# Opening three weight units of the next stage before the barrier of each norm of h, in a four-stage fp32 model kernel on one core

## Chip, cores and metric

One Trainium2 chip, one core. The metric is the device time of one execution in microseconds, lower is better. 0.3% of this kernel's time is about 5.8 us.

## The reference, cut to what matters

The input is one sequence of 512 tokens of width 1024. Four blocks run one after the other on the residual h, and each begins with an RMS norm of h:

```
h = x
h = h + ssd_mixer(rmsnorm(h) ...)                 # stage "ssd"
h = h + gla_mixer(rmsnorm(h) ...)                 # stage "gla"
h = rmsnorm(h, final_norm)                        # the end of the first block
u = rms_norm(h, norm_mix_g)                       # the second block: stages "mixp", "att", "merge"
h = h + (gates0 * conv(u) + gates1 * mla(u)) @ w_out
h = h + cross_attention(rms_norm(h), rms_norm(mem))   # stage "cross"
h = h + relu(rms_norm(h) @ w1)**2 @ w2                # stage "mlp"
out = rms_norm(h)
```

At the end of the gla stage two norms follow each other: `final_norm` (it changes h itself) and the norm of the second block.

## The kernel before

**Tiling.** h is held as 8 row tiles of 128 channels by 512 tokens. Every product with a weight matrix runs in units: one unit is up to 128x1024 weights (8 slices k of 128x128, or 4 slices for 256 output channels). A value is split into a rounded high part and the rest, so one product is three matmuls per slice (`mm3`, lines 63 to 67; low by high, high by low, high by high). A unit with 8 slices is thus 24 matmuls of 512 columns.

**The weight stream.** Units have one global order. SyncE (SP) loads unit n into one of RAW = 2 raw buffers (`load_unit`, L105), once the unit two before it has been split. ScalarE (ACT) rounds it into one of WS = 3 high buffers (`split_hi`, L115), once it has landed and the unit three before it has been multiplied. VectorE (DVE) forms the rest (`split_lo`, L126). TensorE (PE) multiplies it (`stream_products`, L145) into one of SB = 3 PSUM banks in turn, once the tile three before it has been read out. A call for a unit that is already loaded, split or streamed does nothing.

**Stages.** Each stage is one block in which every engine has its own program in a hand-written order. Between stages stand a clearing of semaphores and a barrier of all engines (`stage_semaphores`, L47 to 57), so an engine goes on only when all have come. A stage's loads and splits may reach past its end, into units of the next stage.

**A norm of h between stages.** While the last tiles of h come in, ACT makes u_hi = h * gain (`scale_tile`, L229) and squares h (`square_tile`, L191), DVE makes u_lo (`scale_rest`, L235), and GpSimd (POOL) adds the squares (`add_squares`, L203, L206). The gain is applied before the product; the reciprocal root of the mean square (rstd) is applied when a product is read out of PSUM. `next_products` (L239 to 245) then runs on PE:

- unit nx.n of the next stage, slice by slice as u_lo comes;
- a product of the sum of squares with ones (two passes of an fp32 matmul, L244), which waits for POOL;
- unit nx.n + 1.

Beside that, `next_rough` (L248) has ACT take the root (Ln, Exp) and split unit nx.n + 3, and `next_fine` (L259) has DVE refine it in four steps (`refine_rstd`, L167 to 177) and split unit nx.n + 3. Then comes the barrier. So there are four such places, called A to D here: A from ssd to gla, B from gla to mixp, C from merge to cross, D from cross to mlp.

**gla, where A ends.** Slot (0,0) of PE holds unit nx.n + 1 (query), slot (0,1) unit nx.n + 2 (key), slots (0,2) and (0,3) the first two value units. In slot (0,0) PE also runs the products for the log gates (L1332), with a small weight that SP loads at the stage's start, behind a memset on POOL (L1264 to 1266, L1271). From them ACT and DVE make decays, gated queries and keys, and their high and low parts (L1418 to 1433, L1554 to 1590). DVE reads the first value tile out behind that (L1511), and only then does PE, in slot (0,3), turn that tile (L1343) and run the attention products.

**gla, where B begins.** Place B has its own code. Two sums of squares are kept (c.sumsq and qs), DVE joins them in ks (L1639), PE multiplies both with ones (L1377, L1378), ACT takes two roots (L1475 to 1481), and DVE refines both, one after the other, before the barrier.

**mixp, where B ends.** POOL multiplies the 8 tiles of h by the first norm (L1762), beside DVE. Slot k of DVE reads tile k - 1 out (L1833), splits unit n0 + k + 2 and then does a step of the rotary angles (L1839 to L1861) or, in slots 5 and 7, of the latent norms. ACT squares tile k - 1 (L1794) ahead of its split of unit n0 + k + 2. PE's slot 4 ends with the sums of the latent squares (L1777), and slot 7 with a product with the rotated key (L1783), which needs the sine table and DVE's L1878 to 1884.

Of the kernel before, what the change touches and what calls it, by code (L numbers as in the profile page):

```python
# [21 lines left out]
D = 1024  # L22
KT = D // P
# [142 lines left out]

def refine_rstd(dve, done, n, r, tmp, sums, width, eps=EPS):  # L167
# [71 lines left out]
def next_products(c, pe, nx):  # L239

    stream_products(c, pe, nx.n, lambda j: c.uh[:, j, :], lambda j: c.ul[:, j, :],
                    ready=lambda j: (c.v_rest, nx.v + j + 1))
    pe.wait_ge(c.square_added, nx.squares)
    pe.matmul(c.q[0][:, :], c.ones[:, :], c.sumsq[:, :], start=True, stop=True).then_inc(c.summed, 1)  # L244
    stream_products(c, pe, nx.n + 1, lambda j: c.uh[:, j, :], lambda j: c.ul[:, j, :])
# [159 lines left out]
def ssd_stage(nc, c, A, plan, gain):  # L405
# [8 lines left out]
    with ExitStack() as ctx:  # L414
# [304 lines left out]
        with nc.Block() as block:  # L719
            @block.sync  # L720
            def _(sp):
                for n in range(first, c.next_unit + 4):
                    load_unit(c, sp, n)
# [479 lines left out]
def gla_stage(nc, c, A, plan, gain, gains):  # L1203
# [10 lines left out]
    with ExitStack() as ctx:  # L1214
# [45 lines left out]
        with nc.Block() as block:  # L1260
            @block.sync
            def _(sp):
# [3 lines left out]
                for n in range(first, c.next_unit + 4):  # L1266
# [13 lines left out]
            def _(pe):  # L1280
# [22 lines left out]
                for i, k in slots:  # L1303
# [21 lines left out]
                    if k == 0:  # L1325
# [43 lines left out]
                    if 8 <= k <= 13:  # L1369
                        if k < 13:  # L1370
# [3 lines left out]
                stream_products(c, pe, nx.n, lambda j: c.uh[:, j, :], lambda j: c.ul[:, j, :],  # L1374
                                ready=lambda j: (c.v_rest, nx.v + j + 1))
                pe.wait_ge(s_both, 1)
                pe.matmul(q[0][:, :], c.ones[:, :], c.sumsq[:, :], start=True, stop=True)  # L1377
                pe.matmul(q[1][:, :], c.ones[:, :], ks[:, :], start=True, stop=True).then_inc(c.summed, 1)  # L1378
                stream_products(c, pe, nx.n + 1, lambda j: c.uh[:, j, :], lambda j: c.ul[:, j, :])

            @block.scalar
            def _(act):
# [3 lines left out]
                for i, k in slots:  # L1386
# [4 lines left out]
                    if pi == GH and pk >= 10:  # L1391

                        for j in range(2):
                            final = free_value(c, tile_of(pi, pk) + j)
                            scale_tile(c, act, nx, (pk - 10) * 2 + j, final)
                            square_tile(c, act, (pk - 10) * 2 + j, final)
# [75 lines left out]
                for n in (nx.n + 1, nx.n + 2):  # L1472
# [3 lines left out]
                act.activation(c.sumsq[:, :], q[0][:, :], ACT.Ln, scale=1.0 / D, bias=c.eps[:, 0:1])\  # L1476
                   .then_inc(s_first, 1)
                act.wait_ge(c.rooted, 2 * nx.ones + 1)
                act.activation(c.rstd, c.rstd, ACT.Exp, scale=-0.5).then_inc(c.rooted, 1)
                act.wait_ge(s_first, 1)  # L1480
                act.activation(c.sumsq[:, :], c.sumsq[:, :], ACT.Exp, scale=-0.5).then_inc(s_first, 1)
# [3 lines left out]
            def _(dve):  # L1485
# [151 lines left out]

                dve.wait_ge(c.square_added, nx.squares)
                dve.scalar_tensor_tensor(out=ks[:, :], in0=c.sumsq[:, :], scalar=EPS, in1=qs[:, :], op0=ALU.mult,  # L1639
                                         op1=ALU.add).then_inc(s_both, 1)  # L1640
                for n in (nx.n + 1, nx.n + 2):
                    split_lo(c, dve, n)
                dve.wait_ge(c.rooted, 2 * nx.ones + 2)
                refine_rstd(dve, c.refined, nx.fine, c.rstd, c.newton, q[1][:, :], D, EPS * EPS)
                dve.wait_ge(s_first, 2)
                refine_rstd(dve, c.refined, nx.fine + 4, c.sumsq[:, :], c.newton, q[0][:, :], D)
# [1349 lines left out]
```

## Time and profile before

| | |
|---|---|
| three runs | 1918.66, 1920.49, 1925.13 us; median 1920.49 us |
| the profiled execution | 1918.41 us, span 1916.7 us |
| busy share of the span | PE 92%, weight loads of PE 74%, DVE 62%, ACT 40%, POOL 21% |
| mean granted clock of PE | 0.962 of 2.4 GHz |
| HBM | 135.7 MB read, 72 GB/s over the span |

The profile is one execution, in microseconds from the span's start. In a row of the timeline stand the start, the duration, the engine, the line, the operation, its tiles, how many are merged, and in brackets how long the engine had been idle and what ended that. Matmuls overlap: the duration of one is longer than the distance to the next. "PEq L57" as a releaser is the barrier.

### The profile page before, as it was taken

The numbers are of one execution on the slowest core, as the hardware profiler recorded it, in microseconds if no ns is written. First come the engines' busy times: TensorE is split into PE (matmuls) and PEld (weight loads), VectorE is DVE, ScalarE is ACT, GpSimd is POOL, SyncE is SP. The second block draws the span as 40 slices with busy tenths as digits, with TensorE's granted clock in tenths as the row PEclk, the third lists the DMA queues.
The fourth block names the chain that finished last, engine by engine and source line by source line (L and its number), as shares of the span: only waits on it lengthen the run. The fifth ranks groups of instructions, "written<-read, shape, count | busy, mean of one in ns | idle before, by whom it ended". The sixth has DMA issues, their size and how long they took to land. (4 is left out here: it accounts for less than half of the span.)

```text
span 1916.7 us, 21367 instructions
## 1 busy us (share of the span) xinstructions
PE 1764.0 (92%) x8104; PEld 1424.9 (74%) x8104; DVE 1187.6 (62%) x1580; ACT 773.6 (40%) x1140; POOL 405.8 (21%) x351
## 2 busy tenths in 40 slices
PE   5989999999977989999997799999899999999997
PEld 4767787777755767878785577888678778888886
DVE  6768877887866646474744675777565553434343
ACT  5433443344324344444433344445444442323232
POOL 0444743564363000000000601222031020000001
PEclk9989999999988898999997899999999999999999
DMA  3312222222201312222221232222323223333331
GB/s 98 89 43 58 65 66 66 64 63 73 56 24 33 85 50 66 77 66 77 67 77 37 60 88 58 67 69 58 99 88 99 88 79 99 98 91 97 99 99 67
DMA packets 252188, 139.18 MB, mean 73 GB/s; under 512 B 25965, under 2 KB 246550, under 8 KB 252086
## 3 DMA queue, kind: packets, MB, share of 16 engines
q1 hardware_dynamic: 252086, 137.82, 25.3%
q8 instruction: 65, 1.06, 0.2%
q14 instruction: 37, 0.30, 0.1%
HBM read 135.70 MB, written 2.10 MB: 72 GB/s over the span
## 5 line engine op out<-in xcount | busy, mean ns | idle before, releaser
L65 PE MATMUL stream<-u_lo,weights_hi 128*128 128x512 f32 (+2 forms) x1312 | 528.7, 403 | 20.5 <-DVE h L1028 5.0
L67 PE MATMUL stream<-u_hi,weights_hi 128*128 128x512 f32 (+2 forms) x1312 | 516.6, 394 | 0.0
L66 PE MATMUL stream<-u_hi,weights_lo 128*128 128x512 f32 (+2 forms) x1312 | 516.5, 394 | 0.0
L133 DVE TENSOR_TENSOR weights_lo<-weights_raw,weights_hi 128x1024 fp32r<-128x1024 f32 (+4 forms) x266 | 335.7, 1263 | 287.1 <-ACT weights_hi L123 287.0
L123 ACT ACTIVATE weights_hi<-weights_raw 128x1024 fp32r<-128x1024 f32 (+4 forms) x266 | 268.4, 1010 | 487.8 <-PE stream L67 455.3
L65 PEld LDWEIGHTS stream<-u_lo,weights_hi 128*128 128x128 f32 (+2 forms) x1312 | 249.7, 190 | 87.3 <-issue 18.9
L66 PEld LDWEIGHTS stream<-u_hi,weights_lo 128*128 128x128 f32 (+2 forms) x1312 | 249.3, 190 | 53.9 <-issue 2.7
L67 PEld LDWEIGHTS stream<-u_hi,weights_hi 128*128 128x128 f32 (+2 forms) x1312 | 248.4, 189 | 55.0 <-issue 0.2
L203 POOL COPY h_sum_of_squares<-h_squares 128x512 f32<-128x512 f32 x5 | 3.2, 649 | 829.0 <-ACT h_squares L191 829.0
L65 PE MATMUL stream<-mlp_a_lo,weights_hi 128*128 128x512 f32 x256 | 100.2, 391 | 0.0
L67 PE MATMUL stream<-mlp_a_hi,weights_hi 128*128 128x512 f32 x256 | 99.7, 389 | 0.0
L66 PE MATMUL stream<-mlp_a_hi,weights_lo 128*128 128x512 f32 x256 | 99.6, 389 | 0.0
L736 POOL TENSOR_TENSOR ssd_y<-ssd_y,ssd_state_parts 128x384 f32<-128x384 f32 x32 | 33.0, 1033 | 184.0 <-DVE ssd_state_parts L1045 181.7
L1962 POOL TENSOR_TENSOR mix_conv<-mix_conv,att_tap_products 128x512 f32<-128x512 f32 x30 | 40.2, 1342 | 125.2 <-ACT att_tap_products L2072 123.2
L1059 DVE SCALAR_TENSOR_TENSOR ssd_bc<-stream,params,ssd_bc 128x510 f32<-128x510 f32 (+1 forms) x64 | 48.0, 749 | 28.6 <-ACT ssd_bc L934 26.9
L2841 DVE SCALAR_TENSOR_TENSOR mlp_relu<-stream,h_squares 128x512 f32<-128x512 f32 x32 | 22.1, 691 | 70.0 <-PE stream L67 69.1
L206 POOL TENSOR_TENSOR h_sum_of_squares<-h_sum_of_squares,h_squares 128x512 f32<-128x512 f32 x34 | 48.5, 1427 | 75.4 <-ACT h_squares L191 73.8
L65 PE MATMUL stream<-ssd_y_lo,weights_hi 128*128 128x512 f32 x128 | 53.3, 416 | 8.0 <-DVE ssd_y_lo L1167 5.2
L816 PE MATMUL q<-ssd_m,ssd_x_pair 128*128 128x128 f32 x256 | 37.2, 290 | 22.9 <-DVE ssd_m L1142 22.9
L2137 DVE SCALAR_TENSOR_TENSOR q<-mix_z,params,q 128x512 f32<-128x512 f32 x76 | 57.1, 751 | 1.7
L816 PEld LDWEIGHTS q<-ssd_m,ssd_x_pair 128*128 128x128 f32 x256 | 33.4, 198 | 31.1 <-DVE ssd_m L1142 30.2
L65 PE MATMUL stream<-gla_y_lo,weights_hi 128*128 128x512 f32 x128 | 50.9, 398 | 5.8 <-DVE gla_y_lo L1594 5.8
(472 smaller groups left out, 3185.2 us busy)
## 6 DMA issues: line engine op xcount, KB each, us to landing
weights_raw<-in_w_mlp_dram SPq DMA_DIRECT2D x64, 512.0 KB, 4.0
weights_raw<-in_ssd_w_in_dram SPq DMA_DIRECT2D x48, 512.0 KB, 3.9
weights_raw<-in_gla_w_in_dram SPq DMA_DIRECT2D x40, 512.0 KB, 3.7
weights_raw<-in_w_in_dram SPq DMA_DIRECT2D x29, 512.0 KB, 3.7
weights_raw<-in_ssd_w_out_dram SPq DMA_DIRECT2D x16, 512.0 KB, 3.7
weights_raw<-in_gla_w_out_dram SPq DMA_DIRECT2D x16, 512.0 KB, 3.3
weights_raw<-in_w_out_dram SPq DMA_DIRECT2D x8, 512.0 KB, 3.8
weights_raw<-in_w_xkv_dram SPq DMA_DIRECT2D x8, 512.0 KB, 4.0
```

Source lines behind the costliest of these rows:

```text
L65: pe.matmul(out, lh, rl, start=first, stop=False, skip_group_check=skip)
L66: pe.matmul(out, ll, rh, start=False, stop=False, skip_group_check=skip)
L67: return pe.matmul(out, lh, rh, start=False, stop=last, skip_group_check=skip)
L123: act.activation(w_view(c, n)[0], raw_view(c, n), ACT.Copy).then_inc(c.w_rounded, 1)
L133: dve.tensor_tensor(lo, raw_view(c, n), hi.bitcast(F32), ALU.subtract).then_inc(c.w_split, 1)
L206: pool.tensor_tensor(acc[:, :], acc[:, :], c.sq[:, n % 2, :], ALU.add).then_inc(c.square_added, 1)
L736: pool.tensor_tensor(y[:, p, a], y[:, p, a], parts[:, d * (T - P):(d + 1) * (T - P)], ALU.add).then_inc(s_fin, 1)
L816: last = pe.matmul(q[p][:, t * P:(t + 1) * P], xp[:, t, p, a], mm[:, t % 2, 2 * p + h, :], start=h == 0, stop=h == 1, skip_group_check=True)
L1059: ins = dve.scalar_tensor_tensor(out=dst[:, a:b], in0=src[:, a + o:b + o], scalar=tap(tp, ct), in1=dst[:, a:b], op0=ALU.mult, op1=ALU.add)
L1962: pool.tensor_tensor(acc[:, LAST, :], acc[:, LAST, :], prod[:, e % 2, :], ALU.add)\
L2137: dve.scalar_tensor_tensor(out=dst, in0=src, scalar=par[:, w:w + 1], in1=q[4][:, :], op0=ALU.mult, op1=ALU.add).then_inc(s_tap, 1)
L2841: dve.scalar_tensor_tensor(out=r_[:, m % 2, :], in0=bank(c, t)[:, :], scalar=0.0, in1=c.rstd, op0=ALU.max, op1=ALU.mult).then_inc(c.bank_f ...
```

## The change

At places A, C and D PE now opens two units at once: slices 0 to 6 of unit nx.n, slices 0 to 5 of unit nx.n + 1, the product with ones, and then the slices left over. After that it streams a third unit, nx.n + 2, before the barrier (at C this is a key unit of the memory, 256 columns wide). At B the two units are opened likewise, then half of the third, the two products with ones (the joined one first), and the other half. ACT's split of unit nx.n + 2 moves ahead of the last two squares there, DVE's splits of nx.n + 1 and nx.n + 2 ahead of the join, and the refinement of the first norm moves behind the barrier, into slot 2 of mixp; the steps of the angles in slots 2 and 3 move to slots 3 and 4. POOL's multiplications of h and PE's first latent sum wait for that refinement. SP loads one unit more ahead in each of the stages. In the first round of gla the products for the log gates stand in slot 1 instead of slot 0.

```diff
+def stream_steps(c, pe, n, xh, xl, ks, ready=None):
+    kt, cols, _, _, rows = c.units[n]
+    t = c.tiles_before[n]
+    hi, lo = w_view(c, n)
+    if ks[0] == 0:
+        pe.wait_ge(c.w_split, n + 1)
+        if t >= SB:
+            pe.wait_ge(c.bank_free[t % SB], t // SB)
+    for k in ks:
+        if ready:
+            pe.wait_ge(*ready(k))
+        last = mm3(pe, bank(c, t)[0:rows, :], hi[:, k, 0:rows], lo[:, k, 0:rows], xh(k), xl(k), k == 0, k == kt - 1)
+    if ks[-1] == kt - 1:
+        last.then_inc(c.tile_done, 1)
+        c.streamed = n + 1
...
-def next_products(c, pe, nx):
-    stream_products(c, pe, nx.n, lambda j: c.uh[:, j, :], lambda j: c.ul[:, j, :],
-                    ready=lambda j: (c.v_rest, nx.v + j + 1))
+def next_products(c, pe, nx, third=None):
+    uh, ul = (lambda j: c.uh[:, j, :]), (lambda j: c.ul[:, j, :])
+    ready = lambda j: (c.v_rest, nx.v + j + 1)
+    stream_steps(c, pe, nx.n, uh, ul, range(KT - 1), ready)
+    stream_steps(c, pe, nx.n + 1, uh, ul, range(KT - 2), ready)
     pe.wait_ge(c.square_added, nx.squares)
     pe.matmul(c.q[0][:, :], c.ones[:, :], c.sumsq[:, :], start=True, stop=True).then_inc(c.summed, 1)
-    stream_products(c, pe, nx.n + 1, lambda j: c.uh[:, j, :], lambda j: c.ul[:, j, :])
+    stream_steps(c, pe, nx.n, uh, ul, range(KT - 1, KT), ready)
+    stream_steps(c, pe, nx.n + 1, uh, ul, range(KT - 2, KT), ready)
+    if third:
+        third()
+    else:
+        stream_products(c, pe, nx.n + 2, uh, ul)
...
-                for n in range(first, c.next_unit + 4):
+                for n in range(first, c.next_unit + 5):
                     load_unit(c, sp, n)
...
-                    if k == 0:
+                    if k == (0 if g else 1):
                         if g:
                             pe.wait_ge(s_on, 4 * g)
...
+                stream_steps(c, pe, nx.n, uh, ul, range(KT - 1), ready)
+                stream_steps(c, pe, nx.n + 1, uh, ul, range(KT - 2), ready)
+                stream_steps(c, pe, nx.n, uh, ul, range(KT - 1, KT), ready)
+                stream_steps(c, pe, nx.n + 1, uh, ul, range(KT - 2, KT), ready)
+                stream_steps(c, pe, nx.n + 2, uh, ul, range(KT // 2))
                 pe.wait_ge(s_both, 1)
-                pe.matmul(q[0][:, :], c.ones[:, :], c.sumsq[:, :], start=True, stop=True)
                 pe.matmul(q[1][:, :], c.ones[:, :], ks[:, :], start=True, stop=True).then_inc(c.summed, 1)
-                stream_products(c, pe, nx.n + 1, lambda j: c.uh[:, j, :], lambda j: c.ul[:, j, :])
+                pe.matmul(q[0][:, :], c.ones[:, :], c.sumsq[:, :], start=True, stop=True).then_inc(s_first, 1)
+                stream_steps(c, pe, nx.n + 2, uh, ul, range(KT // 2, KT))
...
                             scale_tile(c, act, nx, (pk - 10) * 2 + j, final)
+                            if pk == 13 and j:
+                                split_hi(c, act, nx.n + 2)
...
+                for n in (nx.n + 1, nx.n + 2):
+                    split_lo(c, dve, n)
                 dve.wait_ge(c.square_added, nx.squares)
                 dve.scalar_tensor_tensor(out=ks[:, :], in0=c.sumsq[:, :], scalar=EPS, in1=qs[:, :], op0=ALU.mult,
                                          op1=ALU.add).then_inc(s_both, 1)
-                for n in (nx.n + 1, nx.n + 2):
-                    split_lo(c, dve, n)
                 dve.wait_ge(c.rooted, 2 * nx.ones + 2)
                 refine_rstd(dve, c.refined, nx.fine, c.rstd, c.newton, q[1][:, :], D, EPS * EPS)
-                dve.wait_ge(s_first, 2)
-                refine_rstd(dve, c.refined, nx.fine + 4, c.sumsq[:, :], c.newton, q[0][:, :], D)
+                c.first_fine = nx.fine + 4
                 split_lo(c, dve, nx.n + 3)
...
+                pool.wait_ge(c.refined, c.first_fine + 4)
                 for m in range(KT):
                     pool.tensor_tensor(c.h[:, m, :], c.h[:, m, :], c.sumsq[:, :], ALU.mult).then_inc(s_first, 1)
...
                         pe.wait_ge(s_sq, (3, 5)[e])
+                        if e == 0:
+                            pe.wait_ge(c.refined, c.first_fine + 4)
...
                     if k == 2:
+                        refine_rstd(dve, c.refined, c.first_fine, c.sumsq[:, :], c.newton, q[0][:, :], D)
+                    if k == 3:
                         dve.wait_ge(s_tb, 3)
...
-                    if k == 3:
+                    if k == 4:
                         dve.wait_ge(s_tb, 7)
...
-                next_products(c, pe, nx)
+                def memory_product():
+                    pe.wait_ge(s_mlo, KT)
+                    stream_products(c, pe, nx.n + 2, lambda j: memh[:, j, :], lambda j: meml[:, j, :], MEM)
+
+                next_products(c, pe, nx, memory_product)
```

## Rows read from the trace of the kernel before

**Rows 1.** The page's first part: busy time and share of each engine.

```profile
PE 1764.0 (92%) x8104; PEld 1424.9 (74%) x8104; DVE 1187.6 (62%) x1580; ACT 773.6 (40%) x1140; POOL 405.8 (21%) x351
```

**Rows 2.** PE's waits: line, releaser, us in total, times, longest.

```profile
PE stream L65 <- PEq L57: 9.7, 4, 3.8
...
PE stream L65 <- DVE u_lo L235: 4.5, 4, 2.5
...
PE q L244 <- POOL h_sum_of_squares L206: 0.4, 2, 0.3
```

**Rows 3.** Timeline of PE at place A.

```profile
621.56 0.39 PE L67 MATMUL stream<-u_hi,weights_hi 128*128 128x512 f32 x1
627.17 3.75 PE L1332 MATMUL q<-gla_gl,gla_w_gates 32*128 32x512 f32 x4 [5.22 <-DMA gla_w_gates<-in_gla_w_gate_dram]
630.85 0.80 PE L65 MATMUL stream<-u_lo,weights_hi 128*128 128x512 f32 x1
...
646.56 0.39 PE L65 MATMUL stream<-u_lo,weights_hi 128*128 128x512 f32 x1
...
647.24 0.39 PE L65 MATMUL stream<-u_lo,weights_hi 128*128 128x512 f32 x1
...
650.49 0.65 PE L1343 MATMUL q<-ident,gla_v 128*128 128x128 f32 x4 [0.37 <-DVE gla_v L1511]
...
654.43 0.48 PE L65 MATMUL stream<-u_lo,weights_hi 128*128 128x512 f32 x1
```

**Rows 4.** Timelines of DVE and POOL at place A.

```profile
614.06 2.30 DVE L133 TENSOR_TENSOR weights_lo<-weights_raw,weights_hi 128x1024 fp32r<-128x1024 f32 x1
...
623.10 0.94 POOL L1271 MEMSET gla_w_gates<- 32x1024 f32 x1 [7.82 <-POOLq L57]
```

**Rows 5.** Stretches: from:to, us, busy us per engine (times), PE's granted clock, DMA.

```profile
628.00:637.00 9.00, 9.00 (x19) 5.50 (x18) 5.04 (x6) 4.84 (x7) 0.00 (x0) 0.53 0.56 152
...
1089.00:1094.00 5.00, 5.00 (x13) 3.89 (x14) 1.76 (x3) 1.52 (x2) 4.77 (x6) 0.51 0.79 189
```

**Rows 6.** Timeline of PE at place B and at the rotated key.

```profile
1074.99 2.07 PE L1377 MATMUL q<-h_sum_of_squares,ones 128*128 128x512 f32 x2 [3.03 <-DVE gla_k L1639]
...
1088.79 0.76 PE L65 MATMUL stream<-u_lo,weights_hi 128*128 128x512 f32 x1 [3.82 <-PEq L57]
...
1130.31 1.13 PE L1783 MATMUL q<-mixp_key_rope,mixp_join 128*128 128x512 f32 x2 [1.85 <-DVE mixp_key_rope L1884]
```

**Rows 7.** Timelines of DVE and POOL at place B and in mixp.

```profile
1080.62 0.69 DVE L170 TENSOR_SCALAR h_squares<-q 128x512 f32<-128x512 f32 x1 [4.55 <-ACT h_squares L1479]
...
1086.43 1.22 DVE L133 TENSOR_TENSOR weights_lo<-weights_raw,weights_hi 128x1024 fp32r<-128x1024 f32 x1
1088.64 0.69 DVE L1833 TENSOR_TENSOR mixp_latent<-stream,h_squares 128x512 f32<-128x512 f32 x1 [0.99 <-PEq L57]
1092.54 1.32 DVE L1839 CAST mixp_angle<-mixp_positions 128x512 f32<-128x512 int32 x1 [3.20 <-DMA mixp_rope_rows<-in_rope_rows_dram]
1093.89 1.40 DVE L1841 TENSOR_SCALAR mixp_angle<-mixp_angle,mixp_rope_rows 128x512 f32<-128x512 f32 x1
...
1107.24 0.48 DVE L1854 TENSOR_SCALAR mixp_angle<-mixp_angle,mixp_rope_rows 128x512 f32<-128x512 f32 x1
...
1129.56 0.69 DVE L1884 TENSOR_TENSOR mixp_key_rope<-mixp_key_rope,h_squares 128x512 f32<-128x512 f32 x1
...
1089.82 11.55 POOL L1762 TENSOR_TENSOR h<-h,h_sum_of_squares 128x512 f32<-128x512 f32 x8
```

**Rows 8.** Timeline of PE at places C and D.

```profile
1459.89 1.02 PE L244 MATMUL q<-h_sum_of_squares,ones 128*128 128x512 f32 x2
...
1467.48 0.36 PE L65 MATMUL stream<-mix_mem_lo,weights_hi 128*128 128x256 f32 x1 [1.08 <-PEq L57]
...
1470.42 0.28 PE L65 MATMUL stream<-mix_mem_lo,weights_hi 128*128 128x256 f32 x1
...
1562.76 0.47 PE L65 MATMUL stream<-u_lo,weights_hi 128*128 128x512 f32 x1 [1.02 <-PEq L57]
```

More of the change, by code:

```diff
@@ L1265, in _ @@
                     sp.dma_start(wg[16 * d:16 * d + 16, d, :], A["gla_w_gate"][0][d]).then_inc(s_gl["w"], 16)
-                for n in range(first, c.next_unit + 4):
+                for n in range(first, c.next_unit + 5):
                     load_unit(c, sp, n)
@@ L1372, in _ @@
                         inter(g, k - 8)
-                stream_products(c, pe, nx.n, lambda j: c.uh[:, j, :], lambda j: c.ul[:, j, :],
-                                ready=lambda j: (c.v_rest, nx.v + j + 1))
+                uh, ul = (lambda j: c.uh[:, j, :]), (lambda j: c.ul[:, j, :])
+                ready = lambda j: (c.v_rest, nx.v + j + 1)
+                stream_steps(c, pe, nx.n, uh, ul, range(KT - 1), ready)
[3 more added lines that the diff above has]
+                stream_steps(c, pe, nx.n + 2, uh, ul, range(KT // 2))
                 pe.wait_ge(s_both, 1)
-                pe.matmul(q[0][:, :], c.ones[:, :], c.sumsq[:, :], start=True, stop=True)
                 pe.matmul(q[1][:, :], c.ones[:, :], ks[:, :], start=True, stop=True).then_inc(c.summed, 1)
-                stream_products(c, pe, nx.n + 1, lambda j: c.uh[:, j, :], lambda j: c.ul[:, j, :])
+                pe.matmul(q[0][:, :], c.ones[:, :], c.sumsq[:, :], start=True, stop=True).then_inc(s_first, 1)
+                stream_steps(c, pe, nx.n + 2, uh, ul, range(KT // 2, KT))
             @block.scalar
@@ L1475, in _ @@
                 act.activation(c.rstd, q[1][:, :], ACT.Ln, scale=1.0 / D, bias=c.eps[:, 1:2]).then_inc(c.rooted, 1)
-                act.activation(c.sumsq[:, :], q[0][:, :], ACT.Ln, scale=1.0 / D, bias=c.eps[:, 0:1])\
-                   .then_inc(s_first, 1)
                 act.wait_ge(c.rooted, 2 * nx.ones + 1)
@@ L1480, in _ @@
                 act.wait_ge(s_first, 1)
+                act.activation(c.sumsq[:, :], q[0][:, :], ACT.Ln, scale=1.0 / D, bias=c.eps[:, 0:1])\
+                   .then_inc(s_first, 1)
+                act.wait_ge(s_first, 2)
                 act.activation(c.sumsq[:, :], c.sumsq[:, :], ACT.Exp, scale=-0.5).then_inc(s_first, 1)
@@ L2235, in _ @@
                 sp.dma_start(rows[:, :, :], A["mem_2"][0].rearrange("(t p) d -> p t d", p=P)).then_inc(s_min, 16)
-                for n in range(n0, n0 + N + 4):
+                for n in range(n0, n0 + N + 5):
                     load_unit(c, sp, n)
@@ L2446, in _ @@
             def _(sp):
-                for n in range(n0, n0 + N + 4):
+                for n in range(n0, n0 + N + 5):
                     load_unit(c, sp, n)
```

## The prediction, made before the changed kernel ran

> **What bounds the kernel now.** I read the page's first part [rows 1]: PE is busy for 92% of the span, so a time that falls has to come out of PE's idle 8% or its clock. PE's waits come next [rows 2]: the four barriers that end in a streamed unit cost 9.7 us, the late rests of u at places B and D 4.5 us, POOL's squares 0.4 us. These are what the change can win. Then I read the timelines around the four places, to see what PE meets after each barrier, and the question there is always the same: does PE set the pace behind the barrier, or does a chain on DVE and ACT that starts at the barrier? Only in the first case is a unit that was streamed early worth its time.
>
> The unit of the sums: one slice (three matmuls of 512 columns) takes 647.24 - 646.56 = 0.68 us [rows 3], so a unit of 8 takes 5.44 us. No work is removed or added by the change, apart from waits; everything below is order.
>
> **Place A, ssd to gla.** Before, PE ends at 621.56 + 0.39 = 621.95 and the next stage starts at 623.10 [rows 3, 4]. Then PE waits until 627.17 for the gate weights, 4.07 us behind the barrier: their DMA is issued inside the stage, behind POOL's memset. The change moves neither, and since unit nx.n + 2 is already streamed, the gate products in slot 1 are still the first thing PE has to do. So that idle of 5.2 us stays, and so does the low clock behind it.
> The third unit is ready in time: its rest is made from 614.06 to 616.36 [rows 4], PE needs it near 621. So PE ends 5.44 us later before the barrier, less about 0.5 us of short waits that the opened units fill [rows 2]: the barrier comes 4.9 us later.
> Behind it a chain starts with the gate products: ACT and DVE make decays, gated q and k and their parts, then DVE reads out the first value tile, and PE turns it at 650.49. PE meets the end of this chain with only 0.37 us of waiting [rows 3]. From the end of the gate products, 630.85, the chain takes 19.6 us. PE filled 19.3 us of it with three units (16.3 us, and 3.0 us for the low clock). Now it has two: 10.9 + 3.0 = 13.9 us, so it waits 19.6 - 13.9 = 5.7 us. Everything behind is fixed to the barrier, which is 4.9 us late: **+4.9 us**.
> Then the clock. A new idle of 5.7 us stands in front of the attention products. After 5.2 us idle PE was granted 0.53 for the 9 us from 628 (9 x 0.47 = 4.2 us lost), after 3.8 us idle 0.51 for the 5 us from 1089 (2.5 us lost) [rows 3, 5, 6]. So the bounds are 0 and 4.2 us; I take the value of the shorter stretch, 2.5 us, because small products stand first: **+2.5 us**.
> The 36 small products from 650.49 to 654.43 are 0.11 us apart, at full clock [rows 3]. The Trainium skill (TensorE: Matmul & The Clock Gate, section "Wait — 56ns, not 53.3ns?") has 128-column matmuls start every 107 ns at 1.2 GHz and every 56 ns at 2.4 GHz. By that these products would lose nothing at 1.2 GHz, since they already run at that distance, and only the matmuls behind them would; that is a rival below.
>
> **Place B, gla to mixp.** Here DVE ends last before the barrier: it starts the refinement at 1080.62, does two of four steps, then a split, 1086.43 + 1.22 = 1087.65 [rows 7]. PE's idle is 2.5 us for u_lo, 3.03 us for the join, 3.82 us at the barrier [rows 2, 6]. After: PE takes slice 6 at about 1068.6, then six slices of the second unit, three leftovers and four of the third, 14 x 0.68 = 9.5 us, to 1078.1; the join, ready at 1074.9, is no longer waited for. Its product alone (1.0 us, as at C [rows 8]) is done at 1079.2, where before both were done at 1078.8 or so. DVE starts at about 1081.0, refines once (4 x 0.72 = 2.9 us) and splits (1.2 us): 1085.1, **2.6 us earlier** than before. ACT's moved split (1.0 us) delays a square, but POOL is still busy with the one before, so the join isn't later.
> Behind this barrier PE doesn't set the pace. From 1088.64 DVE and ACT hand each other read-out, square and two splits slot by slot with the angle steps between, then the latent norm, the sine and the rotated key, which ends at 1130.25; PE waits 1.85 us for it [rows 6, 7]. That chain of 41.6 us never waits for PE, so a unit streamed early gives PE only more to wait. The chain itself changes: + 2.9 us for the refinement in slot 2. Its three angle operations from 1092.54 took 1.32, 1.40 and 1.40 us beside POOL's products, where a like one alone takes 0.48 [rows 7]; POOL now starts only behind the refinement, so they get back about 2.4 us. The same POOL work (11.55 us) then lies beside a later angle step: + 0.9 us. So the chain grows by 1.4 us. Bounds: 0 if the DMA of the angle rows hides more, 3.8 us if nothing is got back. PE's added waits for the refinement cost nothing, since that is done at 12 us behind the barrier, and the latent sum can't start before 14.7. Together -2.6 + 1.4 = **-1.2 us**. PE's idle in this stretch grows by a unit, so the low clock behind the rotated key lasts longer: 0 to 2.5 us, I take **+0.6 us**, because DVE holds PE up again right behind it.
>
> **Place C, merge to cross.** No stall to win but the barrier's 1.08 us. The ones product moves behind six slices of the second unit and ahead of one of the first: 5 x 0.68 = 3.4 us later. Root, refinement and split follow it, and PE restarts 7.6 us after it [rows 8], so at 1470.9. In exchange the 256-column unit, 1470.42 - 1467.48 = 2.9 us, is done before. Behind the barrier all three banks are full, so PE waits for the first read-out (0.7 us, like the 0.69 in [rows 7]), and the earlier load of the fourth unit gives back some of it: **+0.7 us**, bounds 0 and 1.5.
>
> **Place D, cross to mlp.** The waits for u_lo, 1.3 of the 4.5 us of [rows 2], and 0.2 us in front of the ones product are filled. Behind the ones product PE has 11 slices, 7.5 us, which is just the length of root, refinement and split, so PE ends last and the barrier's 1.02 us [rows 8] stays. The full banks cost 0.7 us. **-0.8 us**, bounds -1.5 and 0. The mlp stage behind is bound by PE, so this stays.
>
> **Sum.** 4.9 + 2.5 - 1.2 + 0.6 + 0.7 - 0.8 = +6.7 us. The profiled execution, 1918.4 us, would become 1925.1; it stands 2.1 us under the median, so the forecast is 1920.5 + 6.7 = **1927.2 us**. I count 0.3%, 5.8 us, as what a measurement of this kernel can tell from no change; the forecast lies just beyond it.
>
> **Rivals.**
> - *The attention products don't feel the clock.* The low clock is spent on products that are 0.11 us apart anyway. Then A's clock term is 0.5 us: +4.7, 1925.2 us. This is what the page's spacing would make of it. For it: the measured distance [rows 3]. Against: weight loads of PE may slow too. 0.18.
> - *The clock costs its full bounds*, 4.2 us at A and 2.5 us at B: +10.3, 1930.8 us. For it: the idle at A is longer than any of the two that I have rows for. 0.14.
> - *The chain at A is shorter than before.* Splits of later units stand between its links, and with the fourth unit loaded early they are done while ACT waits; two splits are 2.3 us less, and the idle may then leave the clock at full: 7.4 - 2.3 - 2.5 = 2.6 at A, 1922.4 us, no change. Against: they overlapped DVE work already. 0.12.
> - *The head start is kept (faster).* Its place is the two stretches behind A and B. It decides at A from the point where the chain behind the gate products takes under 13.9 us instead of 19.6, at B where the rotated key comes 5 us earlier. Then A gives -0.5, B -2.6 - 4 = -6.6, with C and D -7.2: 1913.3 us. For it: PE is the busiest engine by far [rows 1]. Against: PE already waits at the end of both chains. 0.11.
>
> **Chances.** 0.45 for the forecast's case, whose own spread puts 0.30 beyond the threshold and 0.15 within. Slower: 0.30 + 0.14 + 0.03 of the first rival = 0.47. Within 0.3%: 0.15 + 0.15 + 0.12 = 0.42. Faster: 0.11. The range leaves out the last rival, and takes in the third down to nearly no change and the second with the upper bounds of B's chain and of C: 1918.5 to 1931.5.
>
> **What would show it.** Right: at A an idle of 5 to 6 us in front of L1343, released by DVE's read-out of the value tile, with a granted clock near 0.5 behind it; the wait for the gate weights unchanged at 5.2 us; at B the barrier 2.6 us earlier, L1841 near 0.5 us, and an idle of 6 us or more in slots 4 to 7 of mixp, the longest in front of L1783; at D no u_lo waits left. Wrong: no new wait at L1343, or a rotated key that comes with PE hardly waiting.

## The result, and the profile after

The changed kernel takes 1928.66 us, the median of 12 runs (1925.15 to 1935.22), against 1917.72 us for the kernel before (12 runs). The ratio is 1.0061, with a 95% interval of 1.0050 to 1.0072: slower, by about 11 us. (A ratio here is estimated from all runs of both kernels; the quotient of the two medians is 1.0057.) The profiled execution after took 1928.18 us (span 1926.5), 9.8 us more span than the one before. One execution of the kernel before, beside experiment 10, took 2393.97 us and is in no ratio.

The page's first part of the changed kernel. Against [rows 1], no engine has noticeably more to do:

```profile
PE 1766.1 (92%) x8104; PEld 1430.2 (74%) x8104; DVE 1189.1 (62%) x1580; ACT 773.8 (40%) x1140; POOL 408.0 (21%) x351
```

PE's waits after. The barriers in a streamed unit have fallen from 9.7 to 3.8 us [rows 2], as the change wants, but a wait for gla_v of 5.9 us and others behind the barriers stand in their place:

```profile
PE q L1369 <- DVE gla_v L1545: 14.1, 4, 5.9
...
PE stream L65 <- DVE weights_lo L133: 6.7, 3, 2.7
...
PE q L1819 <- DVE mixp_key_rope L1922: 4.9, 1, 4.9
...
PE q L1358 <- DMA gla_w_gates<-in_gla_w_gate_dram: 4.3, 1, 4.3
...
PE stream L65 <- DVE mixp_latent L1869: 3.8, 1, 3.8
PE stream L65 <- PEq L57: 3.8, 1, 3.8
```

PE's timeline at place A after, the counterpart of [rows 3]. The turn of the value tile, which was at 650.49 with 0.37 us of waiting, is at 654.37 with 5.94. The products behind it are 0.21 us apart instead of 0.11:

```profile
626.33 0.39 PE L67 MATMUL stream<-u_hi,weights_hi 128*128 128x512 f32 x1
631.06 3.75 PE L1358 MATMUL q<-gla_gl,gla_w_gates 32*128 32x512 f32 x4 [4.34 <-DMA gla_w_gates<-in_gla_w_gate_dram]
...
654.37 1.12 PE L1369 MATMUL q<-ident,gla_v 128*128 128x128 f32 x4 [5.94 <-DVE gla_v L1545]
...
655.83 0.41 PE L65 MATMUL q<-gla_q_lo,gla_k_hi 128*128 128x128 f32 x1
656.04 0.41 PE L66 MATMUL q<-gla_q_hi,gla_k_lo 128*128 128x128 f32 x1
```

POOL's timeline there, with the barrier at 627.79; PE had ended 1.1 us before it:

```profile
627.79 0.94 POOL L1297 MEMSET gla_w_gates<- 32x1024 f32 x1 [12.29 <-POOLq L57]
```

Stretches after, with the columns of [rows 5]. The granted clock is at its lower level of 1.2 GHz for all of 654 to 660, right behind the 5.94 us of idle:

```profile
654.00:660.00 6.00, 5.63 (x27) 5.63 (x28) 3.88 (x5) 0.60 (x1) 0.00 (x0) 0.50 0.52 145
660.00:668.00 8.00, 8.00 (x34) 6.89 (x34) 3.88 (x6) 1.72 (x3) 0.00 (x0) 0.75 0.08 24
```

Timelines of POOL, DVE and PE at place B after, one fence each, against [rows 6, 7]. The barrier is at 1094.80, the first angle steps are fast as predicted, but the three steps of L1888, beside POOL's products, take 5.04 us, where L1850 before took 2.15. First the two rows of the kernel before, from DVE's and POOL's timelines:

```profile
1101.70 2.15 DVE L1850 SCALAR_TENSOR_TENSOR mixp_angle<-mixp_turns,mixp_angle 128x512 f32<-128x512 f32 x3
...
1088.60 0.20 POOL L1752 MEMSET mix_z<- 128x120 f32 x1 [14.39 <-POOLq L57]
```

After:

```profile
1094.80 0.20 POOL L1785 MEMSET mix_z<- 128x120 f32 x1 [12.35 <-POOLq L57]
...
1106.57 12.51 POOL L1796 TENSOR_TENSOR h<-h,h_sum_of_squares 128x512 f32<-128x512 f32 x8 [10.52 <-DVE h_sum_of_squares L194]
```

```profile
1099.29 0.49 DVE L1877 TENSOR_SCALAR mixp_angle<-mixp_angle,mixp_rope_rows 128x512 f32<-128x512 f32 x1
...
1111.66 5.04 DVE L1888 SCALAR_TENSOR_TENSOR mixp_angle<-mixp_turns,mixp_angle 128x512 f32<-128x512 f32 x3
```

```profile
1139.69 2.08 PE L1819 MATMUL q<-mixp_key_rope,mixp_join 128*128 128x512 f32 x2 [4.91 <-DVE mixp_key_rope L1922]
```

Where the 9.8 us arise, by landmarks of the two timelines: 0.2 up to PE's stream on ssd_y_lo ahead of A (592.82 before, 593.03 after); 7.2 from there to the first slice of u at B (1061.85 and 1069.28); 1.95 from there to the rotated key (68.46 and 70.41 us); 0.5 from the key to C's first slice; 0.7 from C's to D's (93.07 and 93.74); -0.8 from D's to the end (369.19 and 368.42).

### The profile page after: what moved, and what is told of

Read it like the earlier page. It is cut to its first block and busy times, and to the rows that moved or that the text cites. A ratio compares the mean times of both kernels' runs of the same rounds, so it can differ in the third digit from the quotient of the medians.

```text
span 1926.5 us, 21368 instructions
## 1 busy us (share of the span) xinstructions
PE 1766.1 (92%) x8104; PEld 1430.2 (74%) x8104; DVE 1189.1 (62%) x1580; ACT 773.8 (40%) x1140; POOL 408.0 (21%) x351
## 5 line engine op out<-in xcount | busy, mean ns | idle before, releaser
L65 PE MATMUL stream<-u_lo,weights_hi 128*128 128x512 f32 (+1 forms) x1312 | 529.1, 403 | 21.5 <-DVE h L1054 5.0
L67 PE MATMUL stream<-u_hi,weights_hi 128*128 128x512 f32 (+1 forms) x1312 | 517.5, 394 | 0.0
L66 PE MATMUL stream<-u_hi,weights_lo 128*128 128x512 f32 (+1 forms) x1312 | 517.2, 394 | 0.0
L65 PEld LDWEIGHTS stream<-u_lo,weights_hi 128*128 128x128 f32 (+1 forms) x1312 | 250.1, 191 | 87.1 <-issue 19.4
L66 PEld LDWEIGHTS stream<-u_hi,weights_lo 128*128 128x128 f32 (+1 forms) x1312 | 249.6, 190 | 54.4 <-issue 2.8
L67 PEld LDWEIGHTS stream<-u_hi,weights_hi 128*128 128x128 f32 (+1 forms) x1312 | 248.8, 190 | 55.1 <-issue 0.2
```

The costliest lines, as they stand in the source:

```text
L65: pe.matmul(out, lh, rl, start=first, stop=False, skip_group_check=skip)
L66: pe.matmul(out, ll, rh, start=False, stop=False, skip_group_check=skip)
L67: return pe.matmul(out, lh, rh, start=False, stop=last, skip_group_check=skip)
```

## The experiments

Each ratio is against runs of the kernel before taken beside it (15 to 29 of them, medians 1917.8 to 1918.5 us). The 0.2 to 0.4% at stake are little more than the intervals, so where two kernels are compared both the medians and the ratios are given.

Four distances serve all of them. **Bar**: from the product that ends PE's idle of 5.2 us for ssd_y_lo to barrier A (592.82 to 623.10 before). **Turn**: from barrier A to PE's first turn of gla_v. **Att**: from there to the same turn of the next group (739.61 before, 748.86 after). **Key**: from barrier B to PE's product on the rotated key. All in us, from one profiled execution each:

```
kernel               bar    turn   idle at turn   att     key
before              30.3    27.4   0.37           89.1    41.7
changed             34.8    26.6   5.94           94.5    44.9
a_no_third          32.8    26.6   1.19           89.8    44.6
a_third_alone       35.2    26.6   5.91           94.5    41.7
a_filled            35.0    26.6   0.56           90.3    44.4
b_restored          34.7    26.6   5.96           94.4    41.7
b_pool_held         36.3    26.1   6.54           93.6    44.8
b_early_refine      35.0    26.6   5.96           94.4    41.4
gates_filled        30.2    27.1   3.04           94.8    41.8
gates_early         30.3    25.0   4.04           94.0    41.7
gates_early_filled  29.9    24.6   2.52           94.9    41.7
best                29.1    26.9   0              89.8    41.4
d_alone             29.6    26.5   1.55           93.1    41.7
c_d_alone           30.3    26.6   1.58           89.4    41.5
```

Up to barrier A the products of the kernels with A as before are the same, and so are those of the kernels with A as changed; within each kind bar still differs by 1.2 and 1.6 us between executions. PE's rows at the start of bar, in before, changed and a_third_alone, one fence each:

```profile
592.82 0.79 PE L65 MATMUL stream<-ssd_y_lo,weights_hi 128*128 128x512 f32 x1 [5.23 <-DVE ssd_y_lo L1167]
```

```profile
593.03 0.80 PE L65 MATMUL stream<-ssd_y_lo,weights_hi 128*128 128x512 f32 x1 [5.23 <-DVE ssd_y_lo L1193]
```

```profile
590.28 0.80 PE L65 MATMUL stream<-ssd_y_lo,weights_hi 128*128 128x512 f32 x1 [5.24 <-DVE ssd_y_lo L1168]
```

**1. Without the third unit at A** (a_no_third).

```diff
-                next_products(c, pe, nx)
+                next_products(c, pe, nx, lambda: None)
...
-                    if k == (0 if g else 1):
+                    if k == 0:
```

> The changed kernel, with the third unit left out ahead of barrier A alone (the next stage streams it, as before) and the gate products back in slot 0; two units stay open at once. Theory 1: the third unit carries all of A's cost, by delaying the barrier and by moving the attention's operand products into an idle in which the clock falls. Then the 5.9 us wait for gla_v is gone, the second L1369 row stands within 1 us of where the kernel before has it, and the time is 7 to 8 us below the changed kernel (10.9 us above the kernel before), so 3 to 4 us above the kernel before: ratio 1.0015 to 1.002. Rival: the order of two open units costs something itself (the ones product of the norm and the last splits later): then A stays 2 us or more late and the ratio is 1.003 or more.

1922.71 us, ratio 1.0016 [1.0004, 1.0028]. Theory 1 holds in the main: 6 us below the changed kernel by the medians, 8.6 by the ratios, and the long idle is gone, in PE's timeline:

```profile
652.51 0.66 PE L1369 MATMUL q<-ident,gla_v 128*128 128x128 f32 x4 [1.19 <-DVE gla_v L1545]
```

But the rival has a share: the barrier is still 2.5 us late. The norm's product with ones now stands behind six slices of the second unit (618.23 instead of 615.33), and DVE's refinement and split that end the stage follow it. From the start of bar to B's first slice A costs 3.0 us here, against 7.2 in the changed kernel.

**2. The third unit alone** (a_third_alone), on the kernel before.

```diff
                 next_products(c, pe, nx)
+                stream_products(c, pe, nx.n + 2, lambda j: c.uh[:, j, :], lambda j: c.ul[:, j, :])
```

> The kernel before, with the third unit streamed ahead of barrier A and nothing else: its gate products stay in slot 0, two units are not open at once. Theory 1: the third unit alone makes A's loss: barrier A 4 to 5 us later, PE idle before the attention's operand products, and those at the lower clock; with the gate products in slot 0 the idle is ahead of them instead, so the loss is 5 to 8 us: ratio 1.0026 to 1.0042. Rival: in the changed kernel the loss comes from gate products moved to slot 1 or from opening two units: then this one costs at most the barrier's delay less the stream it has done already, 0 to 2 us: ratio at most 1.001.

1927.14 us, ratio 1.0057 [1.0043, 1.0071], above the expected 1.0042. The profiled execution is the fastest of the six and shows 4.9 us of span; it was already 2.5 us ahead at the start of bar, before the edit has any effect. From there on it loses 5.0 us up to the barrier, then has 5.91 us of idle and the low clock behind it, and at B's first slice it is 7.75 us later than the kernel before, against 7.2 in the changed kernel. One unit streamed ahead of A is enough to make the whole loss there, and the slot of the gate products, the old one here, has no part in it. The barrier, the turn and the stretch in question:

```profile
625.51 0.94 POOL L1272 MEMSET gla_w_gates<- 32x1024 f32 x1 [13.79 <-POOLq L57]
```

```profile
652.11 1.11 PE L1344 MATMUL q<-ident,gla_v 128*128 128x128 f32 x4 [5.91 <-DVE gla_v L1512]
```

```profile
654.00:660.00 6.00, 6.00 (x29) 6.00 (x29) 1.76 (x3) 0.00 (x0) 0.00 (x0) 0.50 0.65 178
```

**3. The idle at the attention filled** (a_filled), on the changed kernel.

```diff
+                    if k == 3 and g == 0:
+                        for _ in range(24):
+                            pe.matmul(q[4][:, :], c.ident_r[:, :], c.uh[:, 0, :], start=True, stop=True)
```

> The changed kernel, with 24 products of 512 columns added on TensorE ahead of the attention's wait for gla_v in slot 3; their results are overwritten and nobody reads them. They take some 5 us of an idle of 5.9 us. Theory 1: of A's 8.2 us, 4.5 are the lower granted clock of the attention's operand products, for which the idle ahead of them is the cause. Then the granted clock of the stretch behind the wait is near full, the triples of products stand 0.33 us apart instead of 0.64, and the time is 4 to 4.5 us below the changed kernel: ratio 1.003 to 1.0037. Rival: the products are spread by what they wait for or by the access of their weights, not by the clock: then the spacing stays at 0.6 us and the ratio stays at 1.0055 or more. Second rival: the added products run at the low clock themselves, last longer than the wait and delay what is behind: ratio 1.006 or more.

1924.28 us, ratio 1.0025 [1.0015, 1.0034]: theory 1. Useless work on PE makes the kernel faster than the changed one, by 4.4 us by the medians and 6.9 by the ratios; 4 to 4.5 were expected, and the intervals can't tell the three sizes apart. The attention's products stand 0.34 us apart in threes instead of 0.64, and the clock stays full. PE's timeline and the stretch:

```profile
649.49 5.60 PE L1363 MATMUL q<-u_hi,ident_r 128*128 128x512 f32 x24
655.66 0.66 PE L1372 MATMUL q<-ident,gla_v 128*128 128x128 f32 x4 [0.56 <-DVE gla_v L1548]
...
656.43 0.28 PE L65 MATMUL q<-gla_q_lo,gla_k_hi 128*128 128x128 f32 x1
656.77 0.27 PE L65 MATMUL q<-gla_q_lo,gla_k_hi 128*128 128x128 f32 x1
```

```profile
654.00:660.00 6.00, 5.44 (x43) 4.86 (x42) 5.07 (x7) 1.09 (x3) 0.00 (x0) 1.00 0.33 89
```

**4. The idle at the gate weights filled** (gates_filled), on the kernel before: 20 such products ahead of `pe.wait_ge(s_gl["w"], 32)`.

> The kernel before, with 20 products of 512 columns added on TensorE while it waits for the gate weights behind barrier A; their results are overwritten and nobody reads them. In the kernel before the stretch behind that 5.2 us wait has a granted clock of 0.53. Theory 1: the low clock behind the idle costs its products about 4 us there, so filling the idle gives 2 to 4 us: ratio 0.998 to 0.999. Rival: what follows is bound by the other engines' chain (splits and weight loads), not by PE's clock: within 0.5 us of the kernel before: ratio 0.9997 to 1.0003.

1923.03 us, ratio 1.0028 [1.0018, 1.0038]: slower, and neither expectation. The first idle and its low clock were gone, so PE was done with its three units sooner, and met the same chain with 3.04 us of idle instead of 0.37. Now the attention ran at the low clock:

```profile
624.00:636.00 12.00, 12.00 (x49) 8.73 (x48) 4.76 (x7) 5.04 (x8) 1.75 (x4) 1.00 0.52 137
...
650.00:660.00 10.00, 9.99 (x42) 9.51 (x43) 4.49 (x6) 1.68 (x3) 0.00 (x0) 0.50 0.39 107
```

In the kernel before, the low clock of [rows 5] costs almost nothing (turn is 27.4 us with it, 27.1 without): it keeps PE just late enough to meet the chain without an idle. This is the same event as in the changed kernel, made without a single streamed unit.

**5. Barrier B as before** (b_restored), on the changed kernel; the kernel before gives the end of gla, all of mixp and gla's loads (one unit less ahead).

> The changed kernel, with barrier B (the end of the gated stage and the whole mixing stage) as in the kernel before; A, C and D keep the change. Theory 1: B cost 1.9 to 2.4 us by its landmarks, so the time is some 2 us below the changed kernel: ratio 1.0045 to 1.005. Rival: B's landmarks are late only because A's delay shifted them against the loads and splits; then restoring B brings nothing or costs the 1.2 us by which its barrier came earlier: ratio 1.006 to 1.0065.

1926.71 us, ratio 1.0040 [1.0028, 1.0052], and from B's first slice to the key 68.45 us, as before. That is 2.0 us under the changed kernel by the medians and 4.0 by the ratios, and the two intervals touch: the runs agree with B's cost by its landmarks, 1.95 us, but hardly show it by themselves.

**6. POOL held behind the angle steps** (b_pool_held).

```diff
                 pool.wait_ge(c.refined, c.first_fine + 4)
+                pool.wait_ge(s_tb, 7)
```

> The changed kernel, with one wait more: GpSimd starts its products on h only when VectorE's three angle steps (L1888) are done, so that the two engines do not run side by side there. Theory 1: the angle steps took 5.04 us instead of 2.15 because GpSimd ran beside them. Then they take 2.2 us again, the rotated key is ready 2 to 3 us earlier, PE's 4.91 us wait for mixp_key_rope shrinks by as much, and the time is 1.5 to 2.9 us below the changed kernel: ratio 1.0041 to 1.005. Rival: the rotated key is held by GpSimd's products too (they start 2 us later), or PE is next held by the low parts of the weights: then the angle steps are short but the wait moves elsewhere, and the time is within 0.5 us of the changed kernel or above it: ratio 1.0055 or more.

1927.50 us (6 runs), ratio 1.0052 [1.0038, 1.0067], which can't be told from the changed kernel. DVE's timeline gives the reason: L1889 takes 2.14 us, but the steps behind it, now beside POOL, take 1.4 to 1.7 us each, where they took 0.43 to 0.69. The cost has moved, and key stays at 44.8, so the time is the rival's, by steps that it did not name:

```profile
1116.50 2.14 DVE L1889 SCALAR_TENSOR_TENSOR mixp_angle<-mixp_turns,mixp_angle 128x512 f32<-128x512 f32 x3
1118.56 0.68 DVE L1870 TENSOR_TENSOR mixp_latent<-stream,h_squares 128x512 f32<-128x512 f32 x1
1120.90 1.55 DVE L133 TENSOR_TENSOR weights_lo<-weights_raw,weights_hi 128x1024 fp32r<-128x1024 f32 x1 [1.65 <-ACT weights_hi L123]
1122.37 1.51 DVE L1893 TENSOR_SCALAR mixp_angle<-mixp_angle,mixp_rope_rows 128x512 f32<-128x512 f32 x1
1123.91 1.41 DVE L1895 TENSOR_SCALAR mixp_turns<-mixp_angle 128x512 f32<-128x512 f32 x1
1125.36 1.68 DVE L1898 TENSOR_TENSOR mixp_angle<-mixp_angle,mixp_turns 128x512 f32<-128x512 f32 x1
```

**7. The refinement in DVE's idle** (b_early_refine), on the changed kernel.

```diff
-                    if k == 2:
-                        refine_rstd(dve, c.refined, c.first_fine, c.sumsq[:, :], c.newton, q[0][:, :], D)
                     if k == 1:
+                        refine_rstd(dve, c.refined, c.first_fine, c.sumsq[:, :], c.newton, q[0][:, :], D)
                         dve.wait_ge(s_p, 32)
```

> The changed kernel, with VectorE's refinement of the first norm's root moved from slot 2 to slot 1 of the mixing stage, into the 3.0 us in which VectorE waits for the rope rows from memory. GpSimd's products on h start some 10 us sooner, near where the kernel before has them, and are over before or soon after the three angle steps begin. In the changed kernel the stretch from barrier B to PE's product on mixp_key_rope is 44.9 us (before: 41.7), and with GpSimd held back behind the angle steps it was 44.8, since the small steps behind them then took 1.4 to 1.7 us each instead of 0.4 to 0.7. Theory 1: those 3.2 us are the time that VectorE loses beside GpSimd where PE waits for VectorE. Then the stretch is 41.7 to 42.9 us and the time 2 to 3 us below the changed kernel: ratio 1.0045 to 1.005. Rival: the 2.9 us of the refinement itself are the loss, wherever it stands: then the stretch stays at 44 us or more and the ratio at 1.0055 or more.

Key falls to 41.4 us, theory 1. POOL starts 3.6 us behind the barrier instead of 11.8, so the three steps meet only its end and take 3.11 us together. POOL's and DVE's timelines:

```profile
1099.96 12.83 POOL L1796 TENSOR_TENSOR h<-h,h_sum_of_squares 128x512 f32<-128x512 f32 x8 [2.33 <-DVE h_sum_of_squares L194]
```

```profile
1111.69 3.11 DVE L1887 SCALAR_TENSOR_TENSOR mixp_angle<-mixp_turns,mixp_angle 128x512 f32<-128x512 f32 x3
```

The runs don't confirm the time: 1928.78 us (8 runs), ratio 1.0054 [1.0036, 1.0072]. The gain of 3.5 us in key is one of the trace, and an interval of 3.5 us to either side neither confirms nor refutes it; the trace of experiment 10 has it again.

**8. D alone, and C with D** (d_alone, c_d_alone), on the kernel before.

> The kernel before, with the change at D alone (two units open at once, a third streamed, one more unit loaded ahead). By the landmarks D gained 0.9 us: ratio 0.9995. Rival: D gained only because it was shifted against the loads by what went before: ratio 1.000 or more.

> The kernel before, with the change at C and D alone; A and B as before. By the landmarks C cost 0.7 and D gained 0.9 us: together within 0.3 us of the kernel before, ratio 0.9998 to 1.0001. Rival: C's cost of 0.7 us in the changed kernel comes from the delay brought from A and B: then C and D together gain some 0.9 us, ratio 0.9995.

Ratios 0.9999 [0.9990, 1.0009] and 1.0007 [0.9998, 1.0017]: both within what can be told from no change. From D's first slice to the end, all kernels with the change at D take 368.4 to 368.5 us, all without it 369.2 to 369.3: D gives 0.7 to 0.8 us. From C's to D's first slice the changed ones took 93.7 to 93.9 us in five of seven executions (the others 92.35 and 95.22), the unchanged ones 93.0 to 93.3 in five of seven (91.92 and 92.25): C costs about 0.7.
These two kernels are alike up to C, yet their attention was not: behind an idle of 1.55 us d_alone had a clock of 0.69, behind 1.58 us c_d_alone had 1.00:

```profile
648.00:656.00 8.00, 6.45 (x38) 6.37 (x37) 5.05 (x7) 1.66 (x2) 0.00 (x0) 0.69 0.47 129
```

```profile
648.00:656.00 8.00, 6.42 (x47) 5.66 (x47) 6.07 (x9) 2.74 (x4) 0.00 (x0) 1.00 0.43 115
```

**9. The gate weights loaded ahead of barrier A** (gates_early), and the same with 12 added products at the attention (gates_early_filled), on the kernel before. The load stands behind the ssd stage's unit loads, and the memset of the gate weights ahead of it, on POOL, moves into that stage too:

```diff
+                sp.wait_ge(c.wg_zero, 1)
+                for d in range(2):
+                    sp.dma_start(c.wg[16 * d:16 * d + 16, d, :], A["gla_w_gate"][0][d]).then_inc(c.wg_in, 16)
...
+                pool.memset(c.wg[:, :, :], 0.0).then_inc(c.wg_zero, 1)
```

> The kernel before, with the gate weights cleared and loaded during the stage ahead of barrier A instead of behind it. In all ten traces so far the attention's gla_v comes 25.8 to 26.7 us behind barrier A, by a chain that begins with that clearing and loading (the gate products start 3.3 to 4.1 us behind the barrier). Theory 1: the chain is about 3 us shorter, so gla_v comes 3 us sooner; PE is there first, idles some 3 us and does the attention's operand products at the low clock, which costs 4 to 5 us (added products in the first idle alone did just that, 1.0028): ratio 0.9998 to 1.001. Rival: the idle stays short enough to keep the clock, and the 3 us are a gain: ratio 0.998 to 0.999.

> As the kernel with the gate weights loaded early, and 12 products of 512 columns (2.7 us) added on TensorE ahead of the attention's wait in slot 3; their results are overwritten and nobody reads them. Theory 1: both the 3 us of the chain and the clock are kept: 3 to 5 us below the kernel before, ratio 0.9975 to 0.9985. Rival: PE is already the later one at the attention, and the added products delay it: ratio 0.999 or more. Second rival: what is gained at A is given back behind it, at the loads of the following units: ratio 0.9995 to 1.

gates_early: 1921.60 us, ratio 1.0011 [0.9995, 1.0028], as theory 1 has it. The chain is 2.4 us shorter, PE idles 4.04 us for gla_v, and the clock takes the gain. gates_early_filled: 1920.78 us, 1.0006 [0.9992, 1.0021], a miss: the 12 products ended 2.5 us early, and the clock fell all the same:

```profile
641.08 2.88 PE L1337 MATMUL q<-u_hi,ident_r 128*128 128x512 f32 x12
646.48 1.11 PE L1346 MATMUL q<-ident,gla_v 128*128 128x128 f32 x4 [2.52 <-DVE gla_v L1514]
```

**10. What gained, together** (best): A with early gate weights and 20 products, B changed with the early refinement, C as before, D changed.

> The parts that gained, together, on the kernel before: A as before but with the gate weights loaded ahead of the barrier and 20 products of 512 columns (4.5 us; results overwritten, read by nobody) ahead of the attention's wait, since with 12 of them 2.5 us of idle and the low clock were left; B as in the changed kernel with the refinement in slot 1 (from B's first u slice to mixp_key_rope: 67.0 us against 68.5 before and 70.4 changed); C as before; D as in the changed kernel. Theory: A gains the 3 us of the chain if the clock stays full at the attention's products, B 1.5 us, D 0.9 us: 3 to 5 us below the kernel before, ratio 0.9975 to 0.9985. Rival: a clock that falls somewhere behind, at waits of 2.5 us that are left in the gated stage and at B, gives back what the landmarks show in one execution: ratio 0.9995 to 1.001.

1913.77 us (11 runs), ratio 0.9977 [0.9963, 0.9991]: faster than both kernels, about 4 us under the kernel before. By the landmarks the gain is hardly A's: from the start of bar to B's first slice it takes 468.6 us, before 469.0, since the 20 products ended 2.4 us after gla_v was read out. It is B's, 65.4 us from the first slice to the key against 68.5, and D's 0.8. At B the barrier now comes 24.0 us behind the first slice (before 26.75) and the chain takes 41.4. Some 1.6 of these 3.1 us are the clock: in this execution it stayed full behind the wait of 2.5 us for u_lo, in b_early_refine, with the same B, it fell, and the way to the key was 67.0 us.

```profile
644.81 4.70 PE L1372 MATMUL q<-u_hi,ident_r 128*128 128x512 f32 x20
649.35 0.60 PE L1381 MATMUL q<-ident,gla_v 128*128 128x128 f32 x4
```

```profile
1127.31 2.08 PE L1831 MATMUL q<-mixp_key_rope,mixp_join 128*128 128x512 f32 x2 [4.61 <-DVE mixp_key_rope L1933]
```

## Why the prediction was right, and where its steps were off

Forecast 1927.2 us, measured 1928.66; the sum was +6.7, the medians differ by +10.9 and the profiled executions by +9.8. That the time is met more closely than the sum is luck: the forecast started from 1920.5 us, the median of three runs, and over twelve runs the kernel before takes 1917.72. Direction, places and mechanism at A held; the size of A's clock term was off, and B had the wrong sign.

- **A, the barrier (+4.9).** The barrier came 4.5 us later. The working put this on the third unit, and the rows agree: in the changed kernel PE's last product ends 1.1 us before the barrier, DVE's last split 3.05 us before it, so PE is what it waits for. It overlooked a second chain, the later product with ones and what follows it, which by itself brings the barrier 2.5 us later (experiment 1). The third unit by itself brings it 5.0 us later (experiment 2). The two run side by side, so the longer one counts and nothing is added. The gate products waited 3.27 us behind the barrier, not 4.07 (PE's idle ahead of them, forecast unchanged at 5.2 us, was 4.34), and turn is 0.8 us shorter with them: 3.7 us in place of 4.9.
- **A, the idle (5.7 us).** Measured 5.94. The chain behind the barrier is fixed: turn is 26.1 to 27.4 us in every kernel that loads the gate weights behind it, whatever PE does meanwhile.
- **A, the clock (+2.5, bounds 0 to 4.2).** Under-sized. Att grew by 5.4 us, beyond the upper bound. In this execution the group loop behind it gave 1.8 back (322.2 us from the next turn to B's first slice before, 320.4 after), so 3.6 net; but that stretch takes 320.4 to 326.9 us in the fourteen executions, with A changed or not, so what it gave back is this execution's. The step that failed is the choice of the shorter stretch because small products stand first: small products feel the clock in full. The rival by which they don't is refuted, and experiment 3, which changes nothing but the idle ahead, brings att from 94.5 to 90.3 us. The Trainium skill (TensorE: Matmul & The Clock Gate, section "Wait — 56ns, not 53.3ns?") has 107 ns between 128-column matmuls at 1.2 GHz and 56 at 2.4. Here, where each product has weights of its own to load, it was 0.21 and 0.11 us, so the distance read in [rows 3] was no floor. Together A is +7.2 against +7.4 in the sum: the two errors cancel, which is luck.
- **B (-1.2 and +0.6).** Measured +1.95 at the key and +0.5 from there to C's first slice (324.13 and 324.61 us, a stretch that takes 323.9 to 326.8 in the fourteen executions). The barrier's 2.6 us was right at full clock (2.8 us in experiments 1 and 10) but only 1.2 us in the changed kernel, where the wait of 2.47 us for u_lo was followed by a clock of 0.57 from 1077 to 1081. The chain grew by 3.2 us instead of 1.4. The first three angle steps gave back 2.8 us, where 2.4 were counted. The step that failed is the term "the same POOL work then lies beside a later angle step: +0.9": it counted one step like those of [rows 7] and overlooked the three scalar_tensor_tensor steps, which lost 2.9 us by themselves. That stays inside the bound of 3.8, which said what happens if nothing is got back. Experiments 6 and 7 show that the place of POOL's products is the cause, in key; the time of the runs is too blurred to show it.
- **C (+0.7) and D (-0.8)** came as computed: +0.7 and -0.8. At C, PE goes on 4.1 us later, as 3.4 + 0.7 had it. At D one wait for u_lo of 0.54 us is left, which the prediction had gone, and PE's wait in the streamed unit is 1.65 us instead of 1.02.
- **The faster rival** asked whether the head start is kept. It isn't, in no experiment: at A PE waits for gla_v wherever no product fills the idle, and at B it waits longer for the rotated key than before (4.61 us in experiment 10, 1.85 before). What B gains in experiment 10 is the earlier barrier, behind which the chain takes 41.4 us as ever.

Not settled: how large the loss of each part is within some 2 us. The medians, the ratios and the profiled executions of a_filled put its gain over the changed kernel at 4.4, 6.9 and 2.3 us, and those of a_third_alone its loss at 9.2, 10.9 and 4.9 us. The spread between executions of one kernel, with clock falls in some and not in others, is of that size.

## What to carry to other kernels

Work done ahead of a barrier is worth something only if its engine sets the pace behind it; before moving it, find what the engine meets next and whether that chain starts at the barrier. In this kernel an idle added on TensorE could be paid twice, the second time by the clock of the products behind it, so shortening one wait (experiment 4) can cost more than it gives when the next is fixed. When an instruction is moved on VectorE, list what GpSimd runs beside it afterwards, not only beside what it ran before.

## What the runs showed of the hardware

- Ahead of the first group's attention an idle of 2.5 us or more was followed by the low clock in all eight executions that have one, one of 1.6 us in one of two, one of 1.2 us or less in none of four. Att is 89.1 to 90.3 us or 93.1 to 94.9, with nothing between: the step is one of 3 to 6 us, however long the idle was.
- But 2.7 us of idle didn't decide it. The same turn of gla_v comes again in three more groups, where PE idled 2.65 to 2.74 us ahead of it 39 times in the fourteen executions; the clock fell in 29 of them and stayed full in 10. What decided between them no experiment here shows. One of the ten, in the changed kernel, PE's timeline and the stretch behind:

```profile
852.82 0.66 PE L1369 MATMUL q<-ident,gla_v 128*128 128x128 f32 x4 [2.74 <-DVE gla_v L1545]
```

```profile
852.82:860.82 8.00, 8.00 (x54) 7.29 (x55) 8.00 (x9) 2.19 (x4) 0.00 (x0) 1.00 0.48 131
```

- VectorE beside GpSimd's products: scalar_tensor_tensor with two inputs in SBUF 1.68 us instead of 0.71, tensor_tensor 1.68 instead of 0.69, tensor_scalar 1.4 to 1.5 instead of 0.43 to 0.48. The read-out of a PSUM tile (mixp_latent, 0.68 us) lost nothing. The weight split (weights_lo), which here begins near the end of one of GpSimd's products, took 1.24 to 1.55 us instead of 1.22, and then it is GpSimd that waits: the longest of its products took 2.28 us before and 2.25 after, the shortest 1.27. The Trainium skill (SBUF — State Buffer, section "Who interferes with whom") has the two engines share a pair of ports that one instruction holds alone, whichever comes first, and VectorE need it with two inputs in SBUF or in its faster modes. The trace agrees, but for the modes, which it doesn't name.
